# The feed-forward down projection of a two-layer block: eight half-size products or seven

## The reference, cut to what matters

```python
D_MODEL = 1024; SEQ = 1024; D_FF = 4 * D_MODEL
u = rmsnorm(x, g_ffn) @ w_up              # [1024, 4096]
return x + jnp.square(jax.nn.relu(u)) @ w_down   # [1024, 4096] @ [4096, 1024]
...
h = rms_norm(x, attn_norm_2)              # the next layer begins with a norm of this
```

## Time and profile before

| what | value |
|---|---|
| time, median of 3 runs | 2980.0 us (2978.26 to 2988.88) |
| span of the profiled execution | 2985.6 us (its own time is not given apart from its span; it lies inside the range of the runs) |
| PE busy | 2760.9 us, 92% |
| DVE busy | 1460.6 us, 49% |
| ACT busy | 779.7 us, 26% |
| POOL busy | 343.8 us, 12% |
| mean granted TensorE clock | 0.964 |
| up stage, seven-product part | about 978 to 1244 us of the span |
| down stage, first to last matmul | 1244.15 to 1600.66 us |
| next layer's block, first matmul | 1612.49 us |

### The profile page before, as it was taken

The page is one execution under the profiler, slowest core; times in us unless marked ns, Lnnn a source line. Parts: engine busy times, 40 slices in busy tenths (PEclk is TensorE's granted clock), DMA queues, the critical chain, the costliest instruction groups (busy, mean ns, idle before and its releaser), DMA issues. The chain is left out here.

```text
span 2985.6 us, 42973 instructions
## 1 busy us (share of the span) xinstructions
PE 2760.9 (92%) x17116; PEld 2150.3 (72%) x17116; DVE 1460.6 (49%) x2423; ACT 779.7 (26%) x1729; POOL 343.8 (12%) x497
## 2 busy tenths in 40 slices
PE   7998998999999999999999998989999969888886
PEld 5876755888778888788888896777887845555553
DVE  6656487666747656543356643554434441111113
ACT  3244186434014555300003413330012201111112
POOL 1023300000001000000001003440011111111112
PEclk9998999999999999999999998998999979999999
DMA  4130121233632334422234220002102399999997
GB/s 151 44 91 20 57 95 37 92 113 121 207 117 106 106 113 141 179 104 85 85 99 104 46 37 2 2 2 57 49 26 110 124 371 416 419 420 417 413 405 293
DMA packets 156406, 438.50 MB, mean 147 GB/s; under 512 B 18984, under 2 KB 65192, under 8 KB 130608
## 3 DMA queue, kind: packets, MB, share of 16 engines
q1 hardware_dynamic: 140512, 400.47, 37.4%
q10 hardware_dynamic: 5184, 18.48, 1.7%
q0 software_dynamic: 10512, 16.80, 1.5%
HBM read 386.99 MB, written 69.27 MB: 153 GB/s over the span
## 5 line engine op out<-in xcount | busy, mean ns | idle before, releaser
L501 PE MATMUL banks<-split_weights,hT_upper 128*128 128x512 f32 x1536 | 484.5, 397 | 16.4 <-DVE hT_lower L138 8.6
L501 PEld LDWEIGHTS banks<-split_weights,hT_upper 128*128 128x128 f32 x1536 | 292.1, 192 | 79.2 <-issue 15.0
L501 PE MATMUL banks<-split_weights,uT_upper 128*128 128x512 f32 x1024 | 316.8, 391 | 3.1 <-DVE uT_lower L138 3.1
L501 PE MATMUL banks<-split_weights,hT_lower 128*128 128x512 f32 x768 | 303.6, 395 | 0.0
L3711 DVE COPY ex_y<-banks 128x512 f32<-128x512 f32 x36 | 24.9, 692 | 414.9 <-PE banks L3628 414.9
L510 PE MATMUL banks<-hT_upper,split_weights 128*128 128x512 f32 x704 | 221.7, 393 | 6.1 <-DVE split_weights L138 4.4
L501 PEld LDWEIGHTS banks<-split_weights,uT_upper 128*128 128x128 f32 x1024 | 192.6, 188 | 43.3 <-issue 3.5
L501 PE MATMUL banks<-split_weights,uT_lower 128*128 128x512 f32 x512 | 199.8, 390 | 0.0
L3599 PE MATMUL banks<-expert_inner,ex_xT 128*64 128x256 f32 (+1 forms) x1056 | 176.6, 394 | 24.3 <-DMA expert_inner<-in_w_up 10.0
L1955 PE MATMUL banks<-hT_upper,split_weights 128*128 128x512 f32 x576 | 189.0, 389 | 0.0
L138 DVE TENSOR_TENSOR split_weights<-raw_weights,split_weights 128x512 fp32r<-128x512 f32 (+1 forms) x128 | 177.7, 1388 | 4.2 <-ACT split_weights L1975 2.2
(11 more groups left out here) (568 smaller groups left out, 5187.0 us busy)
## 6 DMA issues: line engine op xcount, KB each, us to landing
expert_inner<-in_w_gate SPq DMA_DIRECT2D x33, 1024.0 KB, 19.4
expert_inner<-in_w_up SPq DMA_DIRECT2D x33, 1024.0 KB, 29.7
expert_inner<-in_w_down SPq DMA_DIRECT2D x32, 1024.0 KB, 28.1
raw_weights<-in_w_in SPq DMA_DIRECT2D x28, 1024.0 KB, 6.7
uT_whole<-u_rows ACTq DMA_DIRECT2D x32, 512.0 KB, 5.7
raw_weights<-in_w_down SPq DMA_DIRECT2D x16, 1024.0 KB, 5.1
raw_weights<-in_w_up SPq DMA_DIRECT2D x28, 512.0 KB, 4.1
x_rows<-x SPq DMA_DIRECT2D x24, 512.0 KB, 3.5
```

Source lines behind the costliest of these rows:

```text
L501: last = pe.matmul(bank, acts[x][:, r * KT // 2 + k, m * P:(m + 1) * P].bitcast(F32R), w[y][:, k, :].bitcast(F32R), start=(r == 0 and k == ...
```

## The change

The down product is seen as a 2 by 2 product too: token halves by inner halves (the two 128-row halves of each 256-row block), inner halves by column halves. Seven products P1, P7, P6, P2, P5, P4, P3 (in this order, `pos` = 0 to 6) replace eight. Each is 8 steps (`s`), a step being two slices of 128 inner rows by 4 token tiles by 3 passes = 24 matmuls; in all 7 x 8 x 24 = 1344 matmuls, in 56 steps j = 0 to 55.

- The four sums of activations that four of the products need (s1 to s4) are made by GpSimd in the up stage, four 128x512 instructions a block, from the four result tiles, and stored by SP to a new HBM tensor `u_sums` (1 MB a block). A result tile may now be overwritten only when GpSimd has read it (`sums_taken`). The two plain blocks use four result tiles in place of two.
- The sums of weights are made by DVE in the step that needs them (P7, P6, P5, P4): one more instruction on 128x1024. Those of P7 and P6 are stored to `w_down_sums`, 512 KB a step, and read back by P6 and P4.
- The upper parts are now made by ACT, the lower by DVE, for both operands of a step, into three places (`SLOTS_3`); raw data has three places as well (`RAWS`).
- P6 accumulates in the banks of P1, P3 in those of P5; what P1 and P1+P6 hold is copied out by ACT (`keep`), and GpSimd adds the copies to `x` (16 instructions of 128x512). DVE adds the rest.
- The loads of the down stage (hidden rows or sums, one or two pieces of weights of 512 KB) are all issued by SP, each step three steps ahead; the reload of `x` stands in SP's list between the loads of step 2 and step 3.
- The norm and the next layer's first channel take the tokens 512 to 1023 first.

The diff, cut to its core (left out: the removed down stage, the end of the block in each list, and the changed half order in the next stage):

```diff
     def slot(self, n):
+        if self.more_tiles is not None:
+            return n % 4
         return n % 2 if n < self.N_ORD else (n - self.N_ORD) % 4
 
     def tile(self, n):
+        if self.more_tiles is not None and n < self.N_ORD and self.slot(n) >= 2:
+            return self.more_tiles[self.slot(n) - 2]
         return self.out_tiles[self.slot(n)]
 
     def stores_before(self, n):
 
+        if self.more_tiles is not None:
+            return n // 4
         if n < self.N_ORD:
             return n // 2
         return (n - self.N_ORD) // 4 + (self.N_ORD // 2 if self.slot(n) < 2 else 0)
...
     def wait_tile_free(self, eng, n):
         if self.stores_before(n):
             eng.wait_ge(self.stored[self.slot(n)], 16 * self.stores_before(n))
+        if self.sums_taken is not None and n >= 4:
+            eng.wait_ge(self.sums_taken, 4 * (n // 4) - (1 if n >= self.N_ORD + 4 and n % 4 < 3 else 0))
...
+    BLOCKS = D_FF // HALF
+    HALF_TT = TT // 2
+    LATE = [m + HALF_TT for m in range(HALF_TT)] + list(range(HALF_TT))
+    PER = 2
+    STEPS = BLOCKS // PER
+    RAWS = SLOTS_3 = 3
+    P1, P7, P6, P2, P5, P4, P3 = range(7)
+    WEIGHT_SUM = (P7, P6, P5, P4)
+    KEPT = (P7, P6)
+    ADDED = {P7: 8, P2: 12, P5: 16, P4: 20}
...
+        def weights(pos, s):
+
+            at = slice(PER * s, PER * (s + 1))
+            b11, b12, b21, b22 = (w_halves[h][:, at, n * BANK:(n + 1) * BANK] for h in range(2) for n in range(2))
+            t3, t2 = (kept_dram[k][:, at, :] for k in range(2))
+            return {P1: [b11], P7: [b22, b12], P6: [t3, b11], P2: [b21], P5: [b12, b11], P4: [t2, b21], P3: [b22]}[pos]
+
...
+            def load_step(j):
+                pos, s = divmod(j, STEPS)
+                if j >= RAWS:
+                    sp.wait_ge(made, 2 * (j - RAWS + 1))
+                    if kept_before(j):
+                        sp.wait_ge(t_stored[j % RAWS], 16 * kept_before(j))
+                if pos == P1:
+                    up.wait_stored(sp, PER * (s + 1))
+                elif pos == P7:
+                    for i in range(2):
+                        sp.wait_ge(sums_stored[i], 16 * (PER // 2) * (s + 1))
+                there = raw_there[j % RAWS]
+                sp.dma_start(raw_hidden(j), hidden(pos, s)).then_inc(there, 16)
+                for dst, src in zip(raw_weights(j), weights(pos, s)):
+                    sp.dma_start(dst, src).then_inc(there, 16)
+
+            def store_weight_sum(j):
+                pos, s = divmod(j, STEPS)
+                if pos in KEPT:
+                    sp.wait_ge(summed, sums_before(j))
+                    dst = kept_dram[KEPT.index(pos)][:, PER * s:PER * (s + 1), :]
+                    sp.dma_start(dst, raw_weights(j)[0]).then_inc(t_stored[j % RAWS], 16)
+
+            def store_sums(b):
+                sp.wait_ge(sum_done, 4 * (b + 1))
+                sp.dma_start(sums_dram[:, :, b, :].rearrange("k p n -> p k n"), sum_tiles(b)).then_inc(sums_stored[b % 2], 16)
+
+            def after_first(w):
+                if w == 0:
+                    for b in range(ORD):
+                        store_sums(b)
+                else:
+                    store_sums(ORD + w - 1)
+                if w == W - 1:
+                    sp.wait_ge(up.product, 7 * w + 3)
+                    for j in range(RAWS):
+                        load_step(j)
 
             c.load_chunks(sp, C_FFN + ORD)
+            up.transfers(sp, after_first, None)
+            store_sums(BLOCKS - 1)
+            c.load_chunks(sp, C_IN2 + 1)
             sp.wait_ge(x_in_stored, 16 * TT)
             sp.wait_ge(up.product, 7 * W)
             for m in range(TT):
                 sp.dma_start(x_sb[:, m, :], x_in[m * P:(m + 1) * P, :]).then_inc(x_there, 16)
+            for j in range(RAWS, 7 * STEPS):
+                load_step(j)
+                store_weight_sum(j - 2)
+                if j == P2 * STEPS:
+                    sp.dma_start(norm.gain, gain).then_inc(norm.gain_there, 16)
             c.load_chunks(sp, C_IN2 + 2)
...
+            for pos in range(7):
+                if pos == P6:
+                    pe.wait_ge(kept, 4)
+                elif pos == P2:
+                    pe.wait_ge(added, ADDED[P7])
+                elif pos == P5:
+                    pe.wait_ge(kept, 8)
+                elif pos == P4:
+                    pe.wait_ge(added, ADDED[P2])
+                elif pos == P3:
+                    pe.wait_ge(added, ADDED[P5])
+                for s in range(STEPS - 2 if pos == P3 else STEPS):
+                    pe.wait_ge(made, 2 * (pos * STEPS + s + 1))
+                    for m in range(HALF_TT):
+                        if pos <= P7 and s == 0:
+                            up.wait_bank(pe, first_bank(pos) + m)
+                        last = products(pos, s, m)
+                    last.then_inc(step_done, 1)
+                    if pos == P3 and s >= STEPS - 4:
+                        i = s - (STEPS - 4)
+                        pe.wait_ge(added, ADDED[P5] + 2 * i + 2)
+                        norm.turn(pe, i)
+            pe.wait_ge(made, 2 * 7 * STEPS)
+            for m in range(HALF_TT):
+                for s in (STEPS - 2, STEPS - 1):
+                    last = products(P3, s, m)
+                last.then_inc(tile_done, 1)
+                if m < 2:
+                    norm.turn(pe, m + 2)
...
+            def uppers(j):
+                if j >= SLOTS_3:
+                    act.wait_ge(step_done, j - SLOTS_3 + 1)
+                elif j:
+                    act.wait_ge(up.product, 7 * W - 2)
+                act.wait_ge(raw_there[j % RAWS], landed(j))
+                acts, w = operand(j)
+                nc.scalar.activation(acts[0].bitcast(F32R), raw_hidden(j), ACT.Copy).then_inc(upper_done, 1)
+                if j // STEPS in WEIGHT_SUM:
+                    act.wait_ge(summed, sums_before(j))
+                nc.scalar.activation(w[0].bitcast(F32R), raw_weights(j)[0], ACT.Copy).then_inc(upper_done, 1)
 
...
+                if w == W - 1 and i == 4:
+                    uppers(0)
...
+            def keep(pos):
+                act.wait_ge(step_done, (pos + 1) * STEPS)
+                if pos == P6:
+                    act.wait_ge(pooled, 4)
+                for m in range(HALF_TT):
+                    nc.scalar.activation(product_kept[:, m, :], c.bank(first_bank(pos) + m), ACT.Copy).then_inc(kept, 1)
 
...
+            for j in range(1, 7 * STEPS):
+                uppers(j)
+                pos, s = divmod(j, STEPS)
+                if s == 2 and pos in (P1 + 1, P6 + 1):
+                    keep(pos - 1)
+                if pos == P3 and 3 <= s < 6:
+                    i = s - 3
+                    act.wait_ge(added, ADDED[P5] + i + 1)
+                    norm.square(act, i, x_sb[:, LATE[i], :])
...
+            g = nc.gpsimd
+            for b in range(BLOCKS):
+                a11, a21, a12, a22 = (up.tile(4 * b + i) for i in ((0, 1, 2, 3) if b < ORD else (0, 2, 3, 1)))
+                s1, s2, s3, s4 = (sum_tile(b, k) for k in range(4))
+                if b >= 2:
+                    pl.wait_ge(sums_stored[b % 2], 16 * (b // 2))
+                pl.wait_ge(up.ready, 4 * b + (4 if b < ORD else 3))
+                g.tensor_tensor(s1, a21, a22, ALU.add).then_inc(sum_done, 1)
+                g.tensor_tensor(s3, a11, a21, ALU.subtract).then_inc(sum_done, 1)
+                pl.wait_ge(sum_done, 4 * b + 1)
+                g.tensor_tensor(s2, s1, a11, ALU.subtract).then_inc(sum_done, 1)
+                pl.wait_ge(sum_done, 4 * b + 3)
+                pl.wait_ge(up.ready, 4 * b + 4)
+                g.tensor_tensor(s4, a12, s2, ALU.subtract).then_inc(sum_done, 1)
+
+            def add_kept(half, n):
+                for m in range(HALF_TT):
+                    x = x_tile(half, m, n)
+                    g.tensor_tensor(x, x, product_kept[:, m, :], ALU.add).then_inc(pooled, 1)
+
+            pl.wait_ge(x_there, 16 * TT)
+            pl.wait_ge(kept, 4)
+            add_kept(0, 0)
+            pl.wait_ge(kept, 8)
+            pl.wait_ge(added, ADDED[P7])
+            add_kept(1, 1)
+            add_kept(1, 0)
+            add_kept(0, 1)
             norm.roots(pl)
...
+            def weight_sum(j):
+                if j // STEPS not in WEIGHT_SUM:
+                    return
+                x, y = raw_weights(j)
+                dve.wait_ge(raw_there[j % RAWS], landed(j))
+                if j // STEPS == P4:
+                    v.tensor_tensor(x, y, x, ALU.subtract).then_inc(summed, 1)
+                else:
+                    v.tensor_tensor(x, x, y, ALU.add if j // STEPS == P6 else ALU.subtract).then_inc(summed, 1)
+
+            def lowers(j):
+                for i, (whole, parts) in enumerate(zip((raw_hidden(j), raw_weights(j)[0]), operand(j))):
+                    dve.wait_ge(upper_done, 2 * j + i + 1)
+                    take_lower(v, parts[1], whole, parts[0]).then_inc(made, 1)
 
...
+            def adds(pos):
```

(23 more changed lines are left out.)

250 lines of the change are left out of this document (124 added, 126 removed).

## The result

The changed kernel takes 3012.4 us (median of 4 runs, 3011.4 to 3017.8). The kernel before takes 2981.3 us in the same series (4 runs, 2978.3 to 2988.9). The ratio is 1.0107, 95% interval [1.0092, 1.0123]: 31 us slower, where 6 us faster was forecast, outside the range given (2947 to 2993).

What follows compares the result with a forecast made beforehand. PE was taken to bound the down stage. Gains of 48.3 us less costs of 42.1 us left 6.2 us, so 2980.0 us would become 2974 us, with a range of 2947 to 2993 us for 8 in 10.

Steps and rivals of the forecast that it cites:

- 192 matmuls fewer: Down stage: 1344 matmuls in place of 1536, at 0.2267 us each, save 43.5 us.
- old stall and clock gone: Old down stage: its 3.1 us wait and the 1.7 us of slow clock behind it go, saving 4.8 us.
- start of the up stage, with clock: Up stage's first block: fifth result tile waits for GpSimd, operands come late; 5 us taken, bounds 0 and 12.
- first steps, with clock: Down stage, steps 0 and 1: evictions on DVE 0.7 us and ACT's last work 0.6 us, together 1.3 us.
- gap at step 3, with clock: Step 3's loads queue behind sums, a weight chunk and x: PE stalls 14.5 us, plus 3.3 us of slow clock.
- chain in P7 and P6: Steps 11 to 25: each load waits for a store issued behind the load before; loss 18 us.
- tail: Norm between the last product and the next layer's first matmul: 11.6 us again, bounds 2 us either way.
- I take P = 7.4: Period in us of one load-and-store step in P7 and P6, between bytes (5.1) and a four-load train (7.9).
- the store behind the load becomes the bound: Rival, SP's list in P7 and P6: at P = 8.8 loss 38.9 us, kernel 2995 us; chance 0.13.
- better queue: Rival: next load's packets start while the store lands, P = 6.3, no up-stage loss; 2952 us; chance 0.25.
- three signs that I had set for being wrong: PE waiting in P5 or P4, gap at step 3 under 9 us, or up-stage blocks growing beyond 19 us.
- the bound of 18: Upper bound in us on the stall at step 3, with GpSimd slowed behind DVE.

Runs made afterwards that it cites:

- e8: Changed kernel with GpSimd's four sums of each block replaced by zero fills that read no SBUF; 3001.0 us.
- e6: Changed kernel with stores before loads, weight chunk at step 28, last sums' store and x behind loads, ACT's upper part earlier, steps 0 to 2 loaded earlier; 2957.9 us.
- e1: Changed kernel with the next layer's first weight chunk loaded at step 26, in P2, not ahead of x and step 3; 3012.2 us.
- e3: Changed kernel with the weight chunk at step 26, last sums' store behind step 3's load, x one tile behind each load of steps 3 to 10; 3003.8 us.
- e2: Changed kernel with SP issuing the store of step j-2's weight sum ahead of step j's loads, not behind them; 2977.6 us.
- e10: Changed kernel with the next layer's first weight chunk loaded at step 30, in P2, not ahead of x and step 3; 3007.6 us.

## Why the prediction was wrong

By its own terms, on the bracket, in us:

| term | predicted | measured after | shown by |
|---|---|---|---|
| 192 matmuls fewer | -43.5 | -43.5 | 72 matmuls in 16.32 us, 0.2267 each |
| old stall and clock gone | -4.8 | -4.8 | no such row |
| start of the up stage, with clock | 5 | 6.8 | e8 |
| first steps, with clock | 1.3 | 4.1 + 2.5 | timeline, e6 |
| gap at step 3, with clock | 14.5 + 3.3 | 21.4 + 2.8 | e1, e3 |
| chain in P7 and P6 | 18 | 36.1 | e2 |
| slow clock in its last step, 22 | 0 | 1.6 | starts 1439.84 and 1446.84 |
| tail | 0 | 0.5 | 12.1 for 11.6 |
| sum | -6.2 | +27.5 (bracket: +27.5) | |

**The step that failed** is "I take P = 7.4". P was 8.9 us: ten loads from 1349.13 to 1429.33. The formula itself nearly held: 15 x (8.9 - 5.44) - 11.5 = 40, measured 36.1, and 37.7 with step 22. The 36.1 are 25.6 us of waits and 88.5 - 23.6 - 10 x 5.44 = 10.5 us inside the same periods. Of these some 7.6 are slow clock (five steps of 7.1 to 7.3 us), and 2.9 are no loss of clock: ahead of a wait a step counts to the end of its last matmul, 5.73 us at full clock and not 5.44. The mechanism, issue, four transfers and landing with nothing overlapped, was the right one; its size was not. I had taken the value between the bytes and a train of four loads of 7.9 us. But the bytes alone are no bound of such a chain, and the store is the last of its train: it is issued 1.4 us into the period, and its landing (7.3 us, median from 1350 to 1400) has to end before the next train begins, which is 8.7. The rival "the store behind the load becomes the bound" had the mechanism and the size, P = 8.8, with a chance of 0.13. Its argument against itself, that the train was issued on another queue, was no reason. The rival "better queue" put P at 6.3: that is e2's 6.15, but only with two lines exchanged. What decides could be read in SyncE's list: a load that waits for a store issued behind the loads ahead of it. None of the three signs that I had set for being wrong came, since all three lie outside the chain; what told was the number of waits and their size, eleven of 1.3 to 3.7 us where eight to ten of about 2 were forecast.

**The gap at step 3** was 6.4 us too small. Of its queue of 7.34 MB one chunk was priced at 409 GB/s, and that rate comes from the stretch of the x tiles. The chunk's 1 KB rows pass at 120 GB/s in the stretch above, and e1 puts the chunk at 9.3 us for the 2.6 it was given. The last sums were stored 12.5 us behind the last up product and not 8. Most of that comes from the late loads of step 0: DVE's last two evictions stand in its list behind step 0's lower parts (1256.54 us), so the last tile was ready some 6.7 us behind the product and not 3.1. Then GpSimd's last two sums were 2.3 and 2.2 us, as they met the lower parts of steps 1 and 2 on DVE: the bound of 18 named that, and I did not take it.

**The first steps** were 5.3 us too small. What was left out is that step 0's loads are issued only 8 us ahead of their use (1245.40 us), behind a store of sums in SyncE's list, so that its upper part starts at 1253.17. The clock fell on that wait too.

**What was right**: the count and the price of the matmuls; no wait in P2, P5, P4 and P3; DVE's 2.29 us rows grown to 3.4 beside GpSimd's sums, with the wait of 4.2 us at 984, and 6.8 us in all, the figure that the turns with the clock gave, in part by luck (a wait of 5.1 and 1.7 for the clock were reckoned, 4.2 and some 2.6 came; the 5 taken was lower); that a short slow stretch is covered by the idle time of its period, for the loss with the slow steps in it, 37.7, is not above the 40 that P alone gives, and e2 has it gone with the waits; the lump of adds at about 2 us, once the lead is gone (2.45 in e2).

**Errors in one direction.** All four costs came out higher than the value taken, and three of them are waits behind other transfers in SyncE's queue. Gap and chain do add: what e1, e3 and e10 took out of the gap was still there behind the chain, save for e3's 6.7 us at the start of P7. What e1 and e3 lost again, 9.6 and 9.1 us, went to the one chunk that was moved.

## What to carry to other kernels

Where a ring of buffers is read, changed and stored back, look in the issuing queue for the load that waits on a store, and count the transfers issued between them: the period is all of them and a landing, not the bytes. Issue the store first if its data are ready then. A transfer that is taken out of one gap has to go where the loads have a lead: the same chunk cost 9.6 us at step 26, right behind the chain, and 1.6 at step 30. When a move returns less than it removed, look for where the moved piece now stands before blaming the section between.
